# Second feed-forward of two transformer blocks: three of four weight combinations made by accumulating transfers instead of VectorE subtractions

## What is computed

```python
h2 = rms_norm_2(x, g_ffn)                       # 256 x 2048
x = x + (silu(h2 @ w_gate) * (h2 @ w_up)) @ w_down   # w_gate, w_up: 2048 x 5632, w_down: 5632 x 2048
```

## Time and profile before

| | |
|---|---|
| median of 3 runs | 2479.93 us (2479.49 to 2480.95) |
| profiled execution | 2479.78 us, span 2477.6 us |
| granted TensorE clock, mean | 0.999 |
| busy: PE, VectorE, ScalarE, GpSimd | 2468.1, 1845.4, 1244.0, 41.1 us |
| HBM read, mean over the span | 471.28 MB, 192 GB/s |

### The profile page before, as it was taken

How to read it: one execution, slowest core, us unless ns; L and a number is a source line. 1 busy time by engine, 2 the same in 40 slices (tenths; PEclk the granted TensorE clock), 3 DMA queues, 4 the chain that set the end, 5 groups by cost and what they waited for, 6 DMA issues and landing times.

```text
span 2477.6 us, 30328 instructions
## 1 busy us (share of the span) xinstructions
PE 2468.1 (100%) x11944; PEld 2069.8 (84%) x11944; DVE 1845.4 (74%) x1465; ACT 1244.0 (50%) x1115; POOL 41.1 (2%) x56
## 2 busy tenths in 40 slices
PE   9999999999999999999999999999999999999999
PEld 9988888888888888888888888888888888888887
DVE  5556555899999999987676656557888888888765
ACT  5445444655555555556544443345555555555453
POOL 0000000000000000000000000000000000000000
PEclk9999999999999999999999999999999999999999
DMA  8555455565555555554655555556555555655643
GB/s 273 186 161 164 164 195 184 196 223 200 188 189 197 192 203 201 189 211 153 220 183 190 169 194 183 204 186 222 200 193 200 198 193 202 203 203 199 212 159 114
DMA packets 238108, 476.72 MB, mean 192 GB/s; under 512 B 9974, under 2 KB 10550, under 8 KB 237254
## 3 DMA queue, kind: packets, MB, share of 16 engines
q1 hardware_dynamic: 234390, 460.25, 54.9%
q0 software_dynamic: 3600, 15.25, 1.8%
q10 hardware_dynamic: 32, 0.01, 0.0%
HBM read 471.28 MB, written 4.19 MB: 192 GB/s over the span
## 4 chain that ended last, share of the span: by engine, by line
PE 99%; DVE 0%; issue 0%; ACT 0%; DMA 0%; DVEq 0%; ACTq 0%
PE acc L1954 53%; PE acc L2195 7%; PE acc L2197 7%; PE acc L2196 7%; PE acc L1947 6%; PE aux L2195 5%; PE aux L2197 5%; PE aux L2196 5%; PE aux L1996 1%; PE aux L2264 1%; PE aux L2388 0%; PE acc L2003 0%; PE aux L2064 0%; PE aux L2045 0%; PE aux L2145 0%
## 5 line engine op out<-in xcount | busy, mean ns | idle before, releaser
L1954 PE MATMUL acc<-w_hi,act_hi 128*128 128x512 f32 x1932 | 758.1, 392 | 0.8 <-DVE w_lo L1140 0.8
L1954 PE MATMUL acc<-w_hi,act_lo 128*128 128x512 f32 x1932 | 752.4, 389 | 0.0
L1954 PE MATMUL acc<-w_lo,act_hi 128*128 128x512 f32 x1932 | 751.9, 389 | 0.0
L1134 DVE TENSOR_TENSOR w_lo<-raw,w_hi 128x2048 fp32r<-128x2048 f32 (+1 forms) x192 | 429.0, 2236 | 289.6 <-ACT w_hi L720 289.6
L720 ACT ACTIVATE w_hi<-raw 128x2048 fp32r<-128x2048 f32 (+1 forms) x192 | 359.2, 1871 | 547.0 <-PE acc L1954 468.5
L736 ACT ACTIVATE w_hi<-mem 128x2048 fp32r<-128x2048 f32 x168 | 322.0, 1917 | 255.5 <-PE aux L2197 146.8
L1954 PEld LDWEIGHTS acc<-w_hi,act_hi 128*128 128x128 f32 x1932 | 362.7, 188 | 77.0 <-issue 2.3
L1954 PEld LDWEIGHTS acc<-w_hi,act_lo 128*128 128x128 f32 x1932 | 362.6, 188 | 76.1
L1954 PEld LDWEIGHTS acc<-w_lo,act_hi 128*128 128x128 f32 x1932 | 362.9, 188 | 73.6
L1140 DVE TENSOR_TENSOR w_lo<-mem,w_hi 128x2048 fp32r<-128x2048 f32 x168 | 384.3, 2288 | 53.8 <-ACT w_hi L736 53.6
L730 ACT ACTIVATE w_hi<-raw 128x2048 fp32r<-128x2048 f32 x140 | 268.4, 1918 | 304.3 <-PE acc L1954 164.5
(11 more groups left out here) (192 smaller groups left out, 2120.9 us busy)
## 6 DMA issues: line engine op xcount, KB each, us to landing
raw<-in_w_in SPq DMA_DIRECT2D x104, 1024.0 KB, 5.2
raw<-in_w_ffn_up SPq DMA_DIRECT2D x48, 1024.0 KB, 5.1
mem<-in_w_ffn_down SPq DMA_DIRECT2D x44, 1024.0 KB, 5.2
mem<-in_w_down SPq DMA_DIRECT2D x44, 1024.0 KB, 5.1
mem<-in_w_ffn_up SPq DMA_DIRECT2D x40, 1024.0 KB, 5.0
raw<-in_w_ple_gate SPq DMA_DIRECT2D x32, 1024.0 KB, 5.4
raw<-in_w_gate SPq DMA_DIRECT2D x24, 1024.0 KB, 5.2
raw<-in_w_up SPq DMA_DIRECT2D x24, 1024.0 KB, 5.3
```

Of the source, the lines that this page charges most:

```text
L1134: v.tensor_tensor(w_lo[:, u % SPL, 0:c], raw[:, r % RAW, 0:c], w_hi[:, u % SPL, 0:c], ALU.subtract).then_inc(lo_done, 1)
L1954: mm = pe.matmul(acc[:, s, m, 0:width], x[:, k, c], w, start=start and n == 0, stop=stop and n == 2, skip_group_check=True)
```

## The change

B12 = value quarter 0 is no longer combined by VectorE. GpSimd issues three transfers that add a quarter straight from DRAM to what lies in B12's slot: B12 + B11 for p5, then + B22 for p6, then + B21 for p4. Each waits for the one before and, for the second and third, for the remainder of the step that used the slot (the third also for the third combination). The first waits for B12's plain load. The third combination stays on VectorE (L1154) and now also waits for the second addition. ScalarE's split waits for the additions instead of `form_done`. The token sums get other signs and a fifth member, -A11, for p1; `gate_out` subtracts where it added. The loads of SyncE stay as they are. The first feed-forward (b = 0) is unchanged.

```diff
...
@@ -524,6 +524,7 @@
         FORM_OF = {"p5": 1, "p6": 2, "p7": 3, "p4": 4}
+        ADDED = [1, 2, 4]
         ones_of = lambda steps: [n for n, x in enumerate(steps) if not isinstance(x, str)]
@@ -722,8 +723,12 @@
                 slot = quarter_slot(b, part)
-                if form:
-                    act.wait_ge(form_done[b], times(i, 4, form))
+                if form and b == 0:
+                    act.wait_ge(form_done[0], times(i, 4, form))
+                elif form == 3:
+                    act.wait_ge(form_done[1], times(i, 1, 1))
+                elif form:
+                    act.wait_ge(quarter_added, times(i, 48, 16 * ADDED.index(form) + 16))
                 else:
@@ -898,10 +903,11 @@
 
-                act.wait_ge(sums_done[b], 4)
-                own.order()
-                step(ACT.Copy, act_hi[1 - b][:, KU:3 * KU, :].rearrange("p k t -> p (k t)"),
-                     sums.rearrange("p s n -> p (s n)"), sums_hi[b])
+                n = (4, 5)[b]
+                act.wait_ge(sums_done[b], n)
+                own.order()
+                step(ACT.Copy, act_hi[1 - b][:, KU:KU + 2 * n, :].rearrange("p k t -> p (k t)"),
+                     sums[:, 0:n, :].rearrange("p s n -> p (s n)"), sums_hi[b])
 
@@ -1153,17 +1159,22 @@
 
-            def form1(b, i):
-                form(b, i, B12, B12, B11, 1, None, (B11, B12))
-
-            def form2(b, i):
-                form(b, i, B12, B22, B12, 2, "p5", (B22,))
+            def form1(i):
+                form(0, i, B12, B12, B11, 1, None, (B11, B12))
+
+            def form2(i):
+                form(0, i, B12, B22, B12, 2, "p5", (B22,))
 
             def form3(b, i):
-                form(b, i, B11, B12, B11, 3, "p1", ())
-
-            def form4(b, i):
-                form(b, i, B12, B21, B12, 4, "p6", (B21,))
+                if b == 0:
+                    form(0, i, B11, B12, B11, 3, "p1", ())
+                    return
+                v.wait_ge(lo_done, ended(1, i, "p1"))
+                v.wait_ge(quarter_added, times(i, 48, 32))
+                v.tensor_tensor(quarter(1, B11), quarter(1, B12), quarter(1, B11), ALU.subtract).then_inc(form_done[1], 1)
+
+            def form4(i):
+                form(0, i, B12, B21, B12, 4, "p6", (B21,))
 
@@ -1513,19 +1524,29 @@
                 a21, a22 = quad[:, 0:KU, P:T], quad[:, KU:2 * KU, P:T]
-                s1, s2, s3, s4 = (sums[:, n, :].rearrange("p (k t) -> p k t", k=KU) for n in range(4))
-                for dst, x, y, op in ((s1, a21, a22, ALU.add), (s2, s1, a11, ALU.subtract),
-                                      (s3, a11, a21, ALU.subtract), (s4, a12, s2, ALU.subtract)):
+                s1, s2, s3, s4, s5 = (sums[:, n, :].rearrange("p (k t) -> p k t", k=KU) for n in range(5))
+                if b == 0:
+                    table = ((s1, a21, a22, ALU.add), (s2, s1, a11, ALU.subtract),
+                             (s3, a11, a21, ALU.subtract), (s4, a12, s2, ALU.subtract))
+                else:
+                    table = ((s1, a21, a22, ALU.subtract), (s2, a11, s1, ALU.subtract),
+                             (s3, a21, a11, ALU.subtract), (s4, a12, s2, ALU.subtract))
+                for dst, x, y, op in table:
                     v.tensor_tensor(dst, x, y, op).then_inc(sums_done[b], 1)
                     did(sums_done[b])
                     own.order()
+                if b == 1:
+                    v.tensor_scalar(s5, a11, -1.0, None, ALU.mult).then_inc(sums_done[1], 1)
+                    did(sums_done[1])
 
             def token_rest(b):
 
                 v.wait_ge(sums_hi[b], 1)
                 own.order()
-                at = slice(KU, 3 * KU)
-                v.tensor_tensor(act_lo[1 - b][:, at, :].rearrange("p k t -> p (k t)"), sums.rearrange("p s n -> p (s n)"),
+                n = (4, 5)[b]
+                at = slice(KU, KU + 2 * n)
+                v.tensor_tensor(act_lo[1 - b][:, at, :].rearrange("p k t -> p (k t)"),
+                                sums[:, 0:n, :].rearrange("p s n -> p (s n)"),
                                 act_hi[1 - b][:, at, :].rearrange("p k t -> p (k t)"), ALU.subtract).then_inc(sums_lo[b], 1)
@@ -1535,7 +1556,7 @@
                     v.scalar_tensor_tensor(gate_tok[:, m, :], acc[:, bank, m, :], r_col[:, m:m + 1], gate_tok[:, m, :],
-                                           ALU.mult, ALU.add).then_inc(gate_done[b], 1)
+                                           ALU.mult, (ALU.add, ALU.subtract)[b]).then_inc(gate_done[b], 1)
 
...
@@ -1685,14 +1706,10 @@
                         up_product(g0 + 1, 1, u - u0 - 6)
-                    if u == u0 + 5:
-                        form1(1, 0)
                     if u < u0 + 8 - SPL:
                         remainder(u + SPL)
                     else:
                         rest_step(1, 0, u + SPL - u0 - 8)
-                    if u == u0 + 7:
-                        form2(1, 0)
 
@@ -1704,22 +1721,16 @@
                         f_rest(1, i)
-                    if j == 3:
-                        form4(1, i)
                     if j == 7:
                         add_down(1, 0, low, ended(1, i, DOWN[0]), None if isinstance(i, int) and i == 0 else times(i, 4, 0))
                         add_down(1, 1, high, ended(1, i, DOWN[1]), times(i, 4, 1))
                     if j == 8:
                         gate_out(1, i, b)
-                    if j == 9 and not ends:
-                        form1(1, i + 1)
                     if j == 11:
                         pair_out(1, i, 1 - b)
                         pair_product(i)
                     if j == 12:
                         add_down(1, 2, acc[:, b, :, :] if ends else low, ended(1, i, DOWN[2]), times(i, 4, 2))
-                    if j == 13 and not ends:
-                        form2(1, i + 1)
                     if j == 13 and ends:
@@ -2231,7 +2242,7 @@
                 if x == "p1":
-                    return half_product(*token_half(b, 0, 0), u, both, True)
+                    return half_product(*(token_half(b, 0, 0) if b == 0 else token_sum(b, 4)), u, both, True)
                 if x == "p6":
@@ -2552,6 +2563,27 @@
             norm_factor(6)
+
+            def add_quarter(i, k, name):
+
+                kind, q = QUARTER[k]
+                n = 48 * i + 16 * ADDED.index(FORM_OF[name])
+                if n:
+                    pool.wait_ge(quarter_added, n)
+                pool.dma_start(raw_slot(quarter_slot(1, B12), KU, N), ffn_src(1, kind, q, i + 1),
+                               accum_op=ALU.add).then_inc(quarter_added, 16)
+
+            def add_quarters(i):
+                pool.wait_ge(raw_in[quarter_slot(1, B12)], quarter_count(1, i, B12))
+                add_quarter(i, B11, "p5")
+                pool.wait_ge(lo_done, ended(1, i, "p5"))
+                add_quarter(i, B22, "p6")
+                pool.wait_ge(lo_done, ended(1, i, "p6"))
+                pool.wait_ge(form_done[1], times(i, 1, 1))
+                add_quarter(i, B21, "p4")
+
+            for i in range(PAIRS):
+                add_quarters(i)
             pool.wait_ge(lo_done, T2 + TAIL[1].index(("last", 0)) + 1)
```

More of the change, by code:

```diff
@@ L222, in build_two_blocks @@
         quad = view(6144, 2 * KU, T)
-        sums = view(8192, 4, N)
+        sums = view(8192, 5, N)
         gate_junk = view(4096, N)
@@ L278, in build_two_blocks @@
             twice("form_done"), twice("part_read"), twice("gate_done"), twice("pair_done"), twice("down_added"))
-        gate_acted, val_done = sem("gate_acted"), sem("val_done")
+        gate_acted, val_done, quarter_added = sem("gate_acted"), sem("val_done"), sem("quarter_added")
         BASE2 = 10752
@@ L1584, in slot @@
                         conv_rest(0, 0)
-                        form1(0, 0)
+                        form1(0)
                     if u < R1 - SPL:
@@ L1590, in slot @@
                     if u == u0 + 6:
-                        form2(0, 0)
+                        form2(0)
                 walk(slot, tasks, u0, u0 + 8, first)
@@ L1599, in finish @@
                     if j == 8:
-                        form1(0, i + 1)
+                        form1(i + 1)
                     if j == 9:
@@ L1607, in finish @@
                     if j == 12:
-                        form2(0, i + 1)
+                        form2(i + 1)
                         add_down(0, 2, gates, ended(0, i, DOWN[2]), times(i, 4, 2))
@@ L1620, in ffn1 @@
                         form3(0, 0)
-                        form4(0, 0)
+                        form4(0)
                     if j == 3:
@@ L1646, in ffn1 @@
                         if j == 3:
-                            form4(0, i)
+                            form4(i)
                         if j == 5:
@@ L1657, in ffn1 @@
                     if j == 2:
-                        form4(0, last)
+                        form4(last)
                     if j == 6:
```

## The result

The changed kernel takes 2490.65 us (median of 6 runs, 2489.96 to 2490.98), the kernel before 2480.2 in the same comparison: a ratio of 1.0042, 95% interval 1.0032 to 1.0052. It is 10.5 us slower, where 6.6 were forecast. The profiled execution took 2490.68 us with a span of 2488.9.

The account below looks back on a forecast made before the run. The prediction took the PE to bound the kernel, busy 2468.1 of 2477.6 us. To 2479.78 us it added only 6.6 at the start, giving 2486.4 (2486.5 by the median); likeliest case 2480 to 2493, full range 2479 to 2550.

Parts of the forecast that it names:

- What bounds the kernel, and what goes: Whole kernel: PE-bound; 30 VectorE combinations, 69 us, go beside the PE, worth nothing or at most 0.8 us.
- The token sums at nothing: Before the rounds: a fifth sum (0.72 us) and longer split and remainder cost nothing, covered by VectorE's slack.
- The price of an accumulation: Each GpSimd transfer: 2.7 us fixed plus two passes, 6.2 us; 8.9 alone, 12.0 in traffic.
- In a round: Rounds two to ten: all three additions fit, the second taking 8.9 of 11.7 us; cost nothing, DMA share 0.88.
- New waits of ScalarE on a DMA: Second feed-forward: ScalarE's w_hi and the PE wait on a DMA in the first round alone, some 7 us in sum.
- At the start: First round: B12 lands late and loads compete; the first two additions overrun 17.4 us free, +6.6 us once.
- so both take 12.0: First round, first two additions: 12.0 us each in traffic, midway between whole and half engines, 24.0 together.
- A: Rival, chance 0.25: adding costs no second pass, the first two additions take 15.1 us and everything fits, 2479.1 us.
- B: Rival, chance 0.24: adding costs three or four passes and every round stalls, 2515 or 2593 us.
- C: Rival, chance 0.06: VectorE holds up GpSimd's issue, up to 2.3 us per addition; 11.2 us at the start, 2491.0.
- D: Rival, chance 0.03: whole kernel faster by over 0.2%, needing a PE that runs faster beside a calmer VectorE.

Follow-up runs that it names:

- e2: Changed kernel with all combinations back on VectorE as additions, only the new signs and fifth token sum kept: 2480.26 us, ratio 1.0001 to the kernel before.
- e4: Changed kernel with GpSimd's 30 transfers overwriting B12's slot instead of adding to it: 2482.4 us, ratio 1.001 to the kernel before.
- e5: Changed kernel with the first round's combinations on VectorE and all of B22 added once more, in series, in nine other rounds: 2563.99 us, ratio 1.0338.
- e1: Changed kernel with only the first round's three combinations back on VectorE, the other nine rounds keeping 27 accumulating transfers: 2479.83 us, ratio 0.9999.

## Why the prediction came out as it did

**What bounds the kernel, and what goes: right.** 30 combinations of VectorE went and nothing was gained.

**The token sums at nothing: right as a price, with one side effect missed.** e2 measures them at nothing. The fifth took 0.43 us where 0.72 was put down. But the sums hold back the remainder that frees B12's slot. SyncE's load of B12, at 1691.54 before:

```profile
1692.38 0.37 SPq L608 DMA_DIRECT2D raw<-in_w_up  x1
```

It is 0.84 us later, of which 0.5 are the offset and 0.3 the fifth sum. For VectorE's combination there was room; for a chain through two transfers there is none, and it counts in full: B12 landed at 1697.5, not 1696.6.

**The price of an accumulation: right.** Two passes were taken, 6.2 us; 6.15 measured. 8.9 us alone were worked out; the later rounds show 8.6. The Trainium skill says that a reducing transfer pays for two sources and not for the addition ("Collectives: The Full Stack", section "The bandwidth ceiling: the fold count and why AG ≠ RS ≠ AR"). The size agrees, 2.0 here against its 1.93; that it is the second source and not the addition, no run here shows.

**In a round: right, with one sign missed.** The second addition took 8.6 of 11.7 us and the DMA share came to 0.85, where 0.88 was worked out. Of the 11.7 us the hand-over takes 0.3, so 2.8 were left, as forecast. The first addition took 12.9 us in the round read, not 12.0, and the third 9.9, not 12.0 to 15.1; both had room. New waits of ScalarE on a DMA were forecast for the first round alone, but there are ten, one a round (total, times, longest):

```profile
ACT w_hi L735 <- DMA raw<-in_w_up: 22.7, 10, 12.1
```

Without the first round's 12.1 us that is 1.2 us a round, which the room behind it takes up.

**At the start: the mechanism right, one term mis-sized.** The step that failed is "so both take 12.0": they took 13.7 and 13.1, 26.8 for 24.0. I took the middle between getting the engines whole and getting half, which is a share of two thirds. Of the 13.7 us, 8.6 - 6.15 = 2.45 are fixed, so the service took 11.25 us for 6.15 of work: an estimated share of 55%, close to half. Beside it stand the late B12 (0.8) and the two hand-overs (0.3 each, none in the sum). From GpSimd's first issue on:

1697.74 + 13.7 + 4.2 + 0.3 + 13.1 + 8.7 = 1737.7, against 1737.78 read and 1709.4 + 24.0 = 1733.4 forecast. The 4.4 us are 2.8 of traffic, 0.8 of B12, 0.6 of hand-over, 0.1 in the chain, and 0.1 of rounding. Without the offset of 0.5 they are 3.9, which is the 10.5 measured less the 6.6 forecast.

The sum has no term for the clock, which fell behind both waits. That this cost nothing is luck: p6's slow matmuls end at 1737.66, just before the remainder that the third gate quarter needs, at 1737.72.

**The rivals.** A fell with its premise: an accumulation does cost a second pass. Had it cost none, as in e4, the two would have taken 18.7 us, not the 15.1 of GpSimd's plain loads, and even that was 2.2 us slower. B (three or four passes) fell with the measured 2.0; e5, a second addition twice as long in nine rounds, cost 84 us. C (VectorE holding up GpSimd's issue): all 30 issues took 1.26 to 1.34 us, with VectorE busy 72% of a round, so no sign of it. The argument against it read a window elsewhere: around the load of p_2, from 2335 to 2345 us, VectorE was busy 75% and not over 80. D fell too: nothing became faster.

## What to carry to other kernels

Giving work to accumulating transfers frees the engine but replaces an instruction of 2.3 us by a latency of 9 us in a quiet stretch and 13 to 14 in traffic; it is free only where that latency has a place, and the place is found by reading, for each one, from the event that lets it start to the instruction that needs it. Steady rounds can have the room while the first does not, because there the loads come late and all at once; one row of the DMA share in that stretch tells. The freed engine here was one that nobody waited for, so even with the room found nothing was gained (e1).

## What was not expected

- An accumulation's issue takes GpSimd 1.27 us, a plain transfer's of the same shape 0.75, one with both sides in SBUF 0.84.
- With SyncE's loads queued, the accumulation got an estimated 55% of the engines' time (worked out above), and the bytes moved fell: the windows of the changed kernel (columns as above) show 277 GB/s at a share of over 1 in the stretch in which it was served, against 352 before in the same stretch. The share reads over 1 there, where two queues overlap.

```profile
1700.00:1710.00 10.00, 10.00 (x46) 8.29 (x45) 0.04 (x1) 0.00 (x0) 0.00 (x0) 1.00 1.07 277
1716.00:1720.00 4.00, 3.54 (x8) 2.84 (x9) 4.00 (x4) 0.97 (x1) 1.27 (x1) 0.50 1.05 387
```

- The granted clock is 0.50 in the window that follows the PE's wait of 4.4 us, which is the lower of its two levels, 1.2 GHz; the matmuls there stand 0.43 us apart instead of 0.23. p6's matmuls behind the second wait slow down in the same way. In the changed kernel this cost nothing of its own, since the third gate quarter waited for VectorE until 1737.72 anyway.
